# Encoder layer on one core: the first decay products of the projection as a pair, its last coupling half a tile later, and two repeated products at its end

## The reference

```
h    = rms_norm(x, attn_norm_w)
proj = h @ w_in                       # 1024 x 2944, 23 column tiles of 128
q, k = rms_norm(q), rms_norm(k)       # per head, over 64 columns
rw   = centred_shift(rw, mu_prev, mu_next)
r, k, v, lw_f, lw_b, la_f, la_b, lg = split(rw)
for d in (forward, backward):
    wl    = -softplus(-(w0[d] + tanh(lw) @ w2[d])) - 0.5
    decay = exp(-exp(wl))
    a     = sigmoid(a0[d] + la @ a2[d])
    kd    = k * (1 + (a - 1) * k_a)
    y    += wkv7_scan(r, decay, kd, v, kk, a, reverse=d)
x = x + concat(neighbourhood attention, RWKV, memory attention) @ w_out
x = x + hierarchical mixture of experts
```

## Time and profile before

| what | value |
|---|---|
| median of 3 runs | 1162.17 us (1161.5 to 1168.49) |
| the profiled execution | 1161.79 us, span 1160.1 us |
| PE busy | 1102.6 us, 95% of the span |
| mean granted TensorE clock | 0.988 |
| projection | about 34 to 404 us of the span |
| attention | from 404.8 us |

### The profile page before, as it was taken

How to read it: one execution, slowest core, us unless ns; L and a number is a source line. 1 busy time by engine, 2 the same in 40 slices (tenths; PEclk the granted TensorE clock), 3 DMA queues, 4 the chain that set the end, 5 groups by cost and what they waited for, 6 DMA issues and landing times. The chain is left out here.

```text
span 1160.1 us, 21908 instructions
## 1 busy us (share of the span) xinstructions
PE 1102.6 (95%) x8474; PEld 595.9 (51%) x8474; DVE 554.0 (48%) x1333; ACT 306.2 (26%) x797; POOL 253.2 (22%) x350
## 2 busy tenths in 40 slices
PE   6999999999999988887979999999999999999997
PEld 5534444444344445566964555764444444455553
DVE  4348616799969477854763353761111111111111
ACT  5055121622221177753640222300000000000000
POOL 0300411040000043512440001251455511112221
PEclk9989999999999989999999999999999999999999
DMA  9440253041320267625834921469999999667433
GB/s 344 145 113 26 57 193 84 24 160 58 109 64 19 82 176 178 183 55 169 235 92 172 372 96 59 183 245 414 412 349 368 363 332 367 255 273 299 148 128 117
DMA packets 126741, 217.98 MB, mean 188 GB/s; under 512 B 55428, under 2 KB 90724, under 8 KB 122744
## 3 DMA queue, kind: packets, MB, share of 16 engines
q1 hardware_dynamic: 101512, 135.44, 34.2%
q0 software_dynamic: 17216, 49.84, 12.6%
q10 hardware_dynamic: 7920, 31.46, 7.9%
HBM read 184.92 MB, written 40.82 MB: 195 GB/s over the span
## 5 line engine op out<-in xcount | busy, mean ns | idle before, releaser
L528 PE MATMUL pj_ps<-hT,pj_w 128*128 128x512 f32 x576 | 254.2, 598 | 0.0
L528 PEld LDWEIGHTS pj_ps<-hT,pj_w 128*128 128x128 f32 x576 | 108.5, 191 | 136.0 <-issue 135.4
L1585 PE MATMUL ps_out<-w_out,mixT 128*128 128x512 f32 x256 | 112.3, 594 | 2.0 <-PEq L2819 1.7
L2431 PE MATMUL ex_py<-wd,ex_hT 128*128 128x512 f32 x256 | 113.1, 593 | 0.0
L2580 ACT ACTIVATE ex_sg<-ex_pg 128x512 f32<-128x512 f32 x16 | 9.6, 597 | 269.4 <-PE ex_pg L2485 269.4
L740 DVE RECIPROCAL mixT<-mixT 128x1024 f32<-128x1024 f32 (+1 forms) x11 | 68.9, 6262 | 24.2 <-ACT mixT L660 19.2
L1585 PEld LDWEIGHTS ps_out<-w_out,mixT 128*128 128x128 f32 x256 | 47.9, 190 | 59.4 <-issue 59.3
L2499 PE MATMUL ex_pu<-proj 128*128 128x512 f32 x176 | 78.2, 593 | 0.0
L2485 PE MATMUL ex_pg<-proj 128*128 128x512 f32 x176 | 77.6, 594 | 0.0
L2694 DVE TENSOR_TENSOR ex_hid<-ex_pu,ex_sg 128x512 f32<-128x512 f32 x16 | 11.1, 692 | 136.2 <-PE ex_pu L2499 136.2
L2431 PEld LDWEIGHTS ex_py<-wd,ex_hT 128*128 128x128 f32 x256 | 47.2, 190 | 52.7 <-issue 52.7
(11 more groups left out here) (366 smaller groups left out, 1857.3 us busy)
## 6 DMA issues: line engine op xcount, KB each, us to landing
wd<-in_moe_w_down ACTq DMA_DIRECT2D x15, 2048.0 KB, 9.7
proj<-in_moe_w_gate SPq DMA_DIRECT2D x11, 2048.0 KB, 10.9
proj<-in_moe_w_up SPq DMA_DIRECT2D x11, 2048.0 KB, 12.0
mixT<-in_moe_w_gate SPq DMA_DIRECT2D x5, 2048.0 KB, 11.0
mixT<-in_moe_w_up SPq DMA_DIRECT2D x5, 2048.0 KB, 10.4
pj_w<-in_w_in SPq DMA_DIRECT2D x18, 512.0 KB, 4.1
proj<-in_x SPq DMA_DIRECT2D x16, 512.0 KB, 10.2
products<-pj_unit POOLq DMA_DIRECT2D x4, 2048.0 KB, 10.4
```

The costliest lines, as they stand in the source:

```text
L528: mm = pe.matmul(ps[:, t % 2, half, :], w_tile(t)[:, n, :], s.hT[:, n, half * 512:(half + 1) * 512], start=(n == 0), stop=(n == KD - 1))
L1585: mm = pe.matmul(s.ps_out[:, t % 2, half * 512:(half + 1) * 512], s.mixT[:, k, t * P:(t + 1) * P], s.w_out[:, k, half * 512:(half + 1) * 5 ...
L2431: mm = pe.matmul(py[:, half, :], hT[:, j, :], wd[e % 2][:, j, half * 512:(half + 1) * 512], start=(j == 0), stop=(j == KF - 1))
```

## The change

There are three edits.

1. The two first decay products, `decay(0, 0)` and `decay(1, 0)`, become one `lora_pair(w2, tanh_lw, 0)`. Direction 1 now lies in `ps_n`, which still holds the sums of item 0, so PE waits for `std_ready` 1 first. ACT reads direction 1 from `ps_n`. `item_sums` of the later items waits for `taken` 2, so that it doesn't overwrite the bank.
2. `couplings(1, 1)` moves from `now` 35 to `now` 36, behind the half (17, 1).
3. After the last half, PE waits for `std_ready` 11 and all of `taken` and makes two products of 128x128 with 128x512 from `hT` into `ps_n`. Nothing reads them.

```diff
-            def decay(d, p):
-                lora(w2[d * HD:(d + 1) * HD, p * P:(p + 1) * P], tanh_lw[d * HD:(d + 1) * HD, :])
-
...
                 if n:
+                    pe.wait_ge(taken, 2)
                     pe.wait_ge(std_ready, n)
...
                     item_sums(1)
                     pe.wait_ge(lora_in, 48)
                     pe.wait_ge(tanh_in, 1)
-                    decay(0, 0)
-                    decay(1, 0)
+                    pe.wait_ge(std_ready, 1)
+                    lora_pair(w2, tanh_lw, 0)
...
-                if now in (34, 35):
-                    couplings(now - 34, 1)
+                if now in (34, 36):
+                    couplings((now - 34) // 2, 1)
                 if now in (37, 38):
                     turn_values(1, now - 37)
+            pe.wait_ge(std_ready, 11)
+            pe.wait_ge(taken, rounds)
+            for _ in range(2):
+                pe.matmul(ps_n[:, 0:512], s.hT[:, 0, 0:P], s.hT[:, 0, 0:512], start=True, stop=True)
...
-                src = ps_n[:, :].rearrange("p (a n) -> p a n", a=2) if d and p else ps_g[:, :, :]
+                src = ps_n[:, :].rearrange("p (a n) -> p a n", a=2) if d else ps_g[:, :, :]
```

## The result

The changed kernel takes 0.9931 of the time before, with a 95% interval of 0.9914 to 0.9947: 8 us less, of a median of 1166.1 over 20 runs of before. The forecast was 11.45 us less. The ratio leaves out seven of the changed kernel's 20 runs, which took 1173.7 to 1179.5 us: 1158.4 us is the median of the 13 others, where the median of all 20 is 1160.2. Beside the experiments before has a median of 1165.2 us over 64 runs. The profiled execution after took 1153.87 us, span 1152.1; it is the fastest of the 20.

What follows compares the result with a forecast made beforehand. PE, busy for 95% of the span, was taken to bound the kernel through its waits and the slow clock after them. 5.85 + 3.9 + 1.7 = 11.45 us off 1161.8 gave 1150.3 us, range 1148.0 to 1156.0.

Steps and rivals of the forecast that it cites:

- The pair: First decay products: 3.2 us from a shorter stop and joint products, 2.65 from tile 2 at full clock; 5.85 together.
- The coupling: Last coupling in the projection: its wait goes and products run at full clock, 16.2 us instead of 20.18; 3.9 won.
- Both covers: After the moved coupling: 2.2 us to spare before DVE's mask, 3 us between that mask and PE's `turn_values(1, 0)`.
- the drain: At the moved coupling: a tiling-mode change drains TensorE; the forecast held its price already in the sum.
- The two products: Before attention: cover the stop, leaving about 0.7 of 2.28 us, and keep full clock for three early steps; 1.7 us won.
- the clock still falls at attention's start: Rival: small, thin first products lose the clock, so the third edit gives -0.2 us instead of 1.7; 1152.2 us, chance 0.17.
- the third term: The gain of 1.7 us booked for the two repeated products, from full clock in attention's early steps.
- absorbed: Rival: another engine or a transfer takes up the pair's or coupling's win, about half is left; 1156 us, chance 0.08.
- A fall in the scan or behind it: Slower rival: moved work loses the clock at the scan's stops, 22 us over 70 us of scan; 1173 us, chance 0.04.

Runs made afterwards that it cites:

- e1: The kernel before with only the decay pair (edit 1): 0.9942 of before, median 1157.3 us.
- e3: The kernel before with only the two repeated products (edit 3): 1.0021 of before, median 1167.7 us.
- e2: The kernel before with only the last coupling moved half a tile later (edit 2): 0.9971 of before, median 1161.0 us.
- e8: Edits 1 and 2 without the products, the pair's four products issued direction by direction: 0.9930 of before, median 1157.2 us.
- e11: Edits 1 and 2 with six repeated products instead of two: 0.9963 of before, median 1161.1 us.
- e13: All three edits unchanged, timed a third time: 0.9931 of before, median 1158.6 us.
- e12: Edits 1 and 2 without the products, repeated as a reference on its chip: 0.9933 of before, median 1157.0 us.
- e6: All three edits unchanged, timed again: 0.9944 of before, median 1159.4 us.
- e9: Edits 1 and 2 without the products, repeated as a reference on its chip: 0.9915 of before, median 1154.8 us.
- e4: Edits 1 and 2 without the products, first timing: 0.9919 of before, median 1155.1 us.
- e10: Edits 1 and 2 with one repeated product instead of two: 0.9984 of before, median 1160.9 us.

## Why the prediction was wrong

**The pair: right, 0.3 us short.** Forecast 5.85 us, measured from sums to `key_sums` 81.35 - 63.53 = 17.82 us against 88.89 - 65.50 = 23.39: 5.57 us. The pair took 1.92 us as forecast and tile 2 kept the clock. The stop was 0.99 us and not 0.8: PE's row starts 0.25 us behind the end of ACT's root (64.65 + 0.69 to 65.59), where I had put 0.06 for the semaphore. ACT and DVE followed. Alone the edit brings 6.8 us by its ratio, and the 5.85 lies within the interval (4.3 to 9.2 us).

**The coupling: right for the execution that it was summed on.** Forecast 3.9 us, measured 3.95 in the trace (16.23 against 20.18 us) and 3.4 as an edit alone. Part of this is luck: where the stop kept its clock (e1, e3) the same stretch took 18.55 us, and the edit would bring 2.3. Likewise the pair's 5.57 us would be 3.9 against e3, where the clock came back sooner (21.69 us from sums to `key_sums`). Both stretches in the profile before were at the costly end of what was seen. Both covers came out as worked out (2.1 and 2.9 us for 2.2 and 3), and the drain that the Trainium skill names (TensorEngine Tiling (Array Packing), Tiling Modes) cost nothing beyond the row that held it.

**The two products: this term failed.** I gave them 1.7 us, as three steps of attention at full clock against three at half. The runs show otherwise, in two ways.

First, what the clock is worth there: over the first 16 steps, 35.4 to 35.6 us where it was low for at most 3 us in four profiles (two more have 35.9), 36.2 to 36.3 where it was low for 10. That is 0.7 us and not 1.9. In the profile after, the turnings at 400.43 and 402.76 came 1.2 and 1.5 us sooner than before, counted from attention's first product, so most of the forecast was there; the next one, at 405.89, was only 0.7 us sooner, as PE waited 1.48 us for ACT, which had waited for DVE's row at 403.71. At full clock PE's first two weighings start 1.6 us apart and not 2.7, so that POOL's second transfer comes 0.30 us behind its first. The five profiles with this distance of 1.6 us (after, e2, e8, e11, e13) are the five in which DVE stands for 1.25 to 1.34 us at that step, and the nine others have no such wait there. e12 has none and its next turning comes 12.33 us behind attention's first product, against 12.45 in after, though the one before it came 0.9 us later.

So the step that failed is that I priced full clock for three early steps by the rate of two later ones, with nothing for DVE and POOL; I had written that the first steps hang on DVE and ACT, and didn't follow the chain through them.

Second, the products don't keep the clock reliably. In four profiles with two products it stayed up twice, and twice (e3 and e6) it held across the barrier and fell 4 us later for 7 us; e12 did much the same without any product. So the rival "the clock still falls at attention's start" was right in half of the cases; its reason, small and thin products, was not tested. The rule that I had taken from the Trainium skill (TensorE: Matmul & The Clock Gate, "What's actually happening"), that the monitor runs free of the kernel, agrees with this and with the stop of 2.44 us that cost its clock before and not in e1 and e3.

What the two products cost is less clear. Three comparisons put them at 2.4 us (e3 against before), 3.4 (e6 against e9) and 1.4 (after against e4, on other chips); the fourth at 0 (e13 against e12). Each has an uncertainty of 2.6 to 3.6 us either way. That they don't bring 1.7 us is shown, by e3 and by e6 against e9; that they cost, and by what, is open. The barrier isn't it, as attention starts no later behind ACT's copy.

**The base: lower than it looked.** I summed against the profiled 1161.8 us, near the median of three runs. Over 64 runs before has 1165.2. So the forecast of 1150.3 was low by 3.4 us for this alone, and the other 4.7 us of the miss of 8.1 are the third term (1.7 forecast against a cost of 0 to 3) and the pair's 0.3, within the spread of the ratios. (Against the 1166.1 of the result's own runs of before, the base takes 4.3 us and the rest is 3.8.) A change of -9.75 on the true median would have given 1155.5, inside the range, and edits 1 and 2 alone were measured at 1154.8 to 1157.0. That base was luck of a kind: in the profile that I had, steps 24 to 46 were 3 to 6 us shorter than in any of thirteen others. The profile of before again has the usual 50.7 and still a span of 1160.1, since its scan is 2.7 us shorter, so a single span says little about such stages.

**A misreading.** I wrote that the clock in 40 slices has three dips, the first at the start-up. The earlier trace rows shows two, the third slice (behind the first decay products) and the fifteenth (attention's start); the fall behind the coupling is too short to show in its slice. No number of the sum hangs on it.

**The other rivals.** Nothing was absorbed by ACT, DVE or a transfer in the projection. A fall in the scan or behind it did occur in some executions, with the edits and without: e1 had about 17 us of low clock between 500 and 607 us. It didn't lengthen the scan as far as I feared (97.8 us against 93.5 to 98.7 in all). The range ended at 1156.0, the measured median is 1158.4. The version with edits 1 and 2 alone has the lowest ratios: 0.9919, 0.9915 and 0.9933, about 9 us less than before.

## What to carry to other kernels

A stop of TensorE in a stage where it is the path costs its length and, in some executions, the slow products behind it. Both can be read off rows of the same trace at full clock, and such terms came out to within 0.3 us against the execution that they were read from; in another the same stop can cost 1.6 us less. In a stage where three engines pass work around, a faster TensorE is worth only what the chain leaves over, so the whole round must be followed before a clock gain is booked. And before summing against one profiled execution, ask how much its unsettled stages differ from run to run: here that was as large as the forecast term.

## What the runs showed of the hardware

- Two products on different halves of the array's rows and into different banks overlap even when two of the one are issued before two of the other (e8: first records 0.01 us apart, 1.92 us for all).
- The same stop at the same place keeps or loses the clock from one execution to the next: 2.44 us before the coupling with 15.23 us for the next 32 records in before, 14.00 in e1 and e3.
- With repeated products before a barrier the clock was at 1.00 across it in all six profiles that have them, but in some it fell afterwards: at 1.00 for 4 to 5 us, then about 7 us at 1.2 GHz (e3, e6, e10). Without them it fell within 1 us of attention's first product in seven profiles, and 5 us behind it in the eighth (e12).
- In attention DVE stands for 0.97 to 2.12 us with no releaser each time that POOL issues an indirect transfer 0.30 us behind another: 70 of 70 in thirteen profiles, none of nine in the profile of before. A bracket `<-issue` on DVE's row is not always such a wait: that at 444.85 in after, 0.71 us, ends 0.06 us behind the scores that it reads. Whether POOL's transfers cause the long ones wasn't tested.
